# Copies of the normed rows made by TensorE from a twice-held transposed buffer, with six gathered rows in flight instead of seven

## The chip, the cores and the metric

The program runs on one core of one Trainium2 chip. The metric is the device time of one launch in microseconds (us), the lower the better. All numbers are float32.

## The reference

The kernel computes one step of a one-layer encoder on 1,024 prompt tokens and 32 sample tokens of width 1,024. A layer is attention of two kinds (stick-breaking over all earlier keys, and a 128-wide window), then a feed-forward part called PEER, in which each token picks 8 x 16 = 128 experts out of 16,384. An expert is one row of `u` and one row of `v`. Only PEER matters here:

```python
xn = rms_norm(h, g_ffn)                      # the normed rows
q  = (xn @ w_q).reshape(t, 8, 2, 128)        # queries of eight heads
s1, s2 = q[:, :, 0] @ keys_1.T, q[:, :, 1] @ keys_2.T
# top 16 of s1 and of s2, top 16 of their 256 sums -> idx (t, 8, 16), gate
hid = gelu(einsum('thkd,td->thk', u[idx], xn))
y   = einsum('thk,thkd->td', gate * hid, v[idx])
out = rms_norm(h + y, g_final)
```

## The kernel before, in words

A first phase (`projection_phase`) computes all projections and stores them in DRAM. The second phase (`fused_phase`) is what the change touches. It handles nine tiles of tokens, t = 0 to 8: eight of 128 prompt tokens and a last one of 32 sample tokens (rows of a tile that are shorter are held in four copies).

**The gathers.** `peer_uv` holds for each expert its row of `u` and its row of `v` side by side, 8 KB. One gather (L707, an indirect DMA issued by GpSimd) fetches 128 such rows, 1 MB, one per partition: 32 tokens times 4 of their experts. 32 gathers make a group g, which serves 32 tokens; there are 33 groups, so 1,056 gathers, four groups to a prompt tile. A gather lands in one of `RING` = 7 buffers `uv`.

**The life of a gathered buffer.** GpSimd issues gather n once the product that read gather n - 7 is done (`vmm`, L705). When it has landed, VectorE multiplies its `u` half with `x_rep` and sums (the dot, L893). After two dots ScalarE applies Gelu to them (L829) and writes two 32-column weight tiles `diag`, one per gather (L835). TensorE multiplies these with the `v` halves into `y_acc` (L1327), four matmul calls of 512 columns per pair. Only then is the pair of buffers free.

**`x_rep`.** The dot needs the group's 32 normed rows on all 128 partitions, four copies of each (`COPIES` = 4). Before, the normed rows `xn` are stored to the DRAM scratch `xn2` (L595) and read back by four DMAs of 32 rows for each group (`load_x_rep`, L602), into two buffers used in turn. The gain `g_ffn` is multiplied in on VectorE with a [128, 1024] copy of it that SyncE loads for every tile (L582) into the place of `kT` and `later`.

**The order of the work.** All engines run through the same written-out list of slots n, one slot per gather (`for n in range(FIRST_SLOT, LAST_SLOT)`, L858, L1101, L1334), and each does in each slot what tables such as `STEP_AT`, `ROUTE_AT` and `GROUP_AT` name. Beside the gathers of tile t, the slots hold the attention and the routing of tile t + 1: attention steps every 4 slots (2(t + 1) of them for a prompt tile, 17 for the last), each with scores, suffix sums and values on TensorE, exponentials and a logarithm on ScalarE (`weights`, L745; `softplus`, L731 to L735) and `keep` on VectorE; then windows and a tail (merge, output projection, norm, turning `xn` into `xnT`); then eight heads of routing, one every 12 slots (queries L1275, `exp_gate` L823 on ScalarE, top-16 searches on VectorE). Each engine works strictly in its own order, so a late instruction holds back all that stands behind it. SyncE issues the ordinary DMAs in the same way.

**ScalarE's tables.** An activation needs its function's table. Before, no table is asked for by the program in the slots; a load stands ahead of an activation whenever the table then held lacks its function. It loads for Exp (L745), for Ln after Exp (L735), for Exp in `exp_gate` (L823) and for Gelu (L829). A wait written in the program ahead of an activation is carried by the instruction that follows it.

**PSUM.** `o_sw` (512 columns) collects the window attention of a tile and is read by `merge_window` (semaphore `msw`); between tiles it is unused.

Of the kernel before, what the change touches and what calls it, by code (L numbers as in the profile page):

```python
# [13 lines left out]
P = 128  # L14
# [26 lines left out]
RING = 7  # L41
# [313 lines left out]
LAST_SLOT = GATHERS + 20  # L355
# [4 lines left out]
GROUP_AT = {(g + 1) * TS: g for g in range(GATHERS // TS)}  # L360
FINISH_AT = {min((t + 1) * P, GATHERS): t for t in range(NT + 1)}


def fused_phase(nc, io, w_q, w_out, s_w):

    with ExitStack() as ctx:
        def sb(name, shape, dt=F32):
# [12 lines left out]
        g_out = sb("g_out", [P, DK])  # L380
        g_final = sb("g_final", [P, DM])
# [14 lines left out]
        g_ffn = part(4, 6)  # L396
# [3 lines left out]
        xnT = sb("xnT", [P, DK, P])  # L400
# [38 lines left out]
                   msw ssq mean2 guess2 mA mB tm mTe op x_in h h_out ssh meanh guessh g_in xn xn_out tx xTe  # L439
# [4 lines left out]
        S_X = [sem(f"x_rep{i}") for i in range(2)]  # L444
# [43 lines left out]
        def _(sync):  # L488
# [5 lines left out]
            for k0, g in ((0, "norm_sb_out"), (4, "norm_swa_out")):  # L494
                sync.dma_start(g_out[:, k0:k0 + 4], io[g].rearrange("o (k p) -> p (o k)", p=P),
                               allow_slow_non_contiguous=True).then_inc(S["const"], 16)
# [83 lines left out]
            def load_g(t):  # L580
                hold(sync, S["pvw"], 4 * t + 4)
                sync.dma_start(g_ffn, io["norm_ffn"].partition_broadcast(P)).then_inc(S["g_in"], 16)  # L582

# [8 lines left out]

            def store_xn(t):
                hold(sync, S["xn"], t + 1)
                sync.dma_start(io["xn2"][tokens_of(t), :], xn[0:rows_of(t), :]).then_inc(S["xn_out"], 16)  # L595

            def load_x_rep(g):
                hold(sync, S["xn_out"], (g // 4 + 1) * 16)
                if g >= 2:
                    hold(sync, S["dot"], (g - 1) * TS)  # L600
                for c in range(COPIES):
                    sync.dma_start(x_rep[c * TS:(c + 1) * TS, g % 2, :], io["xn2"][g * TS:(g + 1) * TS, :]  # L602
                                   ).then_inc(S_X[g % 2], 16)

# [26 lines left out]
            for n in range(FIRST_SLOT, LAST_SLOT):  # L631
# [20 lines left out]
                if (at := WINDOW_AT.get(n - 7)) and at[1] == 3:  # L652
                    load_g(at[0])
# [4 lines left out]
                if (t := TAIL_AT.get(n - 19)) is not None:  # L658
                    store_xn(t)
                    if t == 0:  # L660
                        load_x_rep(0)
                        load_x_rep(1)
                        load_h(0)
                if (g := GROUP_AT.get(n - 2)) is not None and g + 2 < GATHERS // TS:
                    load_x_rep(g + 2)
                if (t := FINISH_AT.get(n - 14)) is not None:
                    store_y(t)
                    if t < NT:
                        load_h(t + 1)
# [7 lines left out]
        def _(pool):  # L677
            nc.gpsimd.memset(q_pad[:], 0.0).then_inc(S["zeroed"], 1)
            hold(pool, S["const"], 13 * 16)
# [32 lines left out]
        def _(act):  # L712
# [4 lines left out]

            def z_of(t, e):
# [3 lines left out]
            def softplus(t, e):  # L722
# [7 lines left out]
                view = soft[0:scores.shape[0], 0:scores.shape[1]]  # L730
                nc.scalar.activation(view, scores, ACT.Abs)  # L731
# [5 lines left out]
            def weights(t, e):  # L737
# [4 lines left out]
                if e == 0 and t:  # L742
                    act.wait_ge(S["xn_out"], t * 16)
                scores = z_of(t, e)
                nc.scalar.activation(probs[0:scores.shape[0], 0:scores.shape[1]], scores, ACT.Exp).then_inc(S["a"], 1)  # L745
# [28 lines left out]
            def merged_guess(t):  # L774
                rows = rows_of(t)
                act.wait_ge(S["mean2"], t + 1)
                rsqrt_guess(nc, act, stat[0:rows, 1, :], stat[0:rows, 2, :], stat[0:rows, 3, :]).then_inc(S["guess2"], 1)
# [13 lines left out]
            def h_guess(t):  # L791
                rows = rows_of(t)
                act.wait_ge(S["meanh"], t + 1)
# [624 lines left out]
```

## Time and profile before

| | |
|---|---|
| median of 3 runs | 3738.09 us (3716.6 to 3742.26) |
| profiled execution: its own time | 3744.33 us |
| profiled execution: span, first to last instruction | 3742.7 us |
| busy PE / DVE / ACT / POOL | 2630.0 / 2236.5 / 1467.8 / 1390.8 us |
| bytes moved, mean rate | 1236.71 MB, 330 GB/s |
| queue of the gathers / the ordinary DMAs | 1122.51 MB, 76.8% / 111.69 MB, 9.4% of 16 DMA engines' span |
| granted TensorE clock, mean | 0.825 of full |

The engines are PE (TensorE), PEld (its weight loads), DVE (VectorE), ACT (ScalarE), POOL (GpSimd) and SP (SyncE). "Busy" is time in which an instruction of the engine runs. "DMA share" is the mean busy share of the core's 16 DMA engines in a stretch; over short stretches it can come out slightly above 1. The first phase and the routing of the first tile end at about 459 us, when the first gather is issued; from there to the end the gathers run. In the page's division of the span in 40 slices, the DMA line shows 9 tenths or more in nearly every slice from about 650 us on.

### The profile page before, as it was taken

The page shows a single profiled execution, that of the slowest core. Times are in us where ns is not written, and L with a number is a line of the kernel's source. Part 1 is how long each engine was busy: PE and PEld are TensorE (multiplying, and loading weights), DVE is VectorE, ACT ScalarE, POOL GpSimd, SP SyncE. Part 2 cuts the span into 40 slices and gives each one's busy share as a digit, 9 for nine tenths or more (in the row PEclk, how much of TensorE's full clock was granted, in tenths as well). Part 3 has the DMA queues.
Part 4 walks back from the last instruction along what each step waited for, and adds up shares of the span by engine and source line. Part 5 has one row for each costly group of instructions (what it writes and reads, how often), then busy time and mean ns, then how long its engine had stood idle before and what let it go on. Part 6 is the DMA issues. An engine that isn't in the chain of part 4 may idle for free.

```text
span 3742.7 us, 40304 instructions
## 1 busy us (share of the span) xinstructions
PE 2630.0 (70%) x11692; PEld 1123.9 (30%) x11692; DVE 2236.5 (60%) x5671; ACT 1467.8 (39%) x3224; POOL 1390.8 (37%) x1363
## 2 busy tenths in 40 slices
PE   7997666667666875777677666776677766667665
PEld 4553442223222321232223222332233224322111
DVE  2010365676667666676576656775766665665675
ACT  1000134225423642364246524653466435552222
POOL 0000014444445344434433344344433433344443
PEclk9998778778878887887879788888888778778787
DMA  6222259999999999999999999999989999999997
GB/s 224 83 80 81 75 212 355 378 401 345 367 391 392 336 383 390 376 344 372 382 368 345 365 391 355 361 335 387 374 343 346 372 377 352 354 367 385 373 386 312
DMA packets 256792, 1236.71 MB, mean 330 GB/s; under 512 B 30304, under 2 KB 99712, under 8 KB 120384
## 3 DMA queue, kind: packets, MB, share of 16 engines
q0 software_dynamic: 156416, 1122.51, 76.8%
q1 hardware_dynamic: 100160, 111.69, 9.4%
q8 instruction: 91, 1.49, 0.2%
q14 instruction: 125, 1.02, 0.1%
HBM read 1205.98 MB, written 32.70 MB: 331 GB/s over the span
## 4 chain that ended last, share of the span: by engine, by line
PE 25%; DMA 22%; DVE 19%; issue 9%; ACT 7%; DVEq 4%; POOL 2%; ACTq 2%; SPq 0%; POOLq 0%
DMA f_uv<-peer_uv,f_idx 18%; PE f_y_acc L1327 12%; DVE f_uv L893 6%; PE f_q_ps L1275 4%; PE f_z L1252 4%; DMA f_work<-cache_sb_kT 3%; POOL f_uv L707 2%; ACT L829 1%; PE f_z L1165 1%; ACT f_diag L835 1%; DMA f_work<-scratch_nat 1%; ACT L735 1%; ACTq L732 1%; ACT L823 1%; ACTq L833 1%
## 5 line engine op out<-in xcount | busy, mean ns | idle before, releaser
L707 POOL DMA_INDIRECT f_uv<-peer_uv,f_idx x1056 | 1210.7, 1147 | 1866.6 <-PE f_y_acc L1327 1624.5
L1327 PE MATMUL f_y_acc<-f_uv,f_diag 128*32 128x512 f32 x4224 | 1318.0, 753 | 598.5 <-ACT f_diag L835 517.8
L893 DVE CUSTOM_DVE_ANT_0 f_uv<-f_uv,f_x_rep 128x1024 f32<-128x1024 f32 x1056 | 1292.8, 1227 | 696.5 <-DMA f_uv<-peer_uv,f_idx 690.7
L1327 PEld LDWEIGHTS f_y_acc<-f_uv,f_diag 128*32 128x32 f32 x4224 | 238.8, 125 | 1272.0 <-ACT f_diag L835 678.6
L829 ACT ACTIVATE f_act_hid<-f_hid 128x2 f32<-128x2 f32 x528 | 107.0, 203 | 1309.2 <-DVE f_hid L893 1293.8
L1275 PE MATMUL f_q_ps<-w_q,f_xnT 128*128 128x256 f32 x1152 | 286.4, 405 | 28.3 <-DVE f_cut L1013 24.4
L835 ACT ACTIVATE f_diag<-f_gate_fold,f_act_hid 128x32 f32<-128x32 f32 x1056 | 281.7, 313 | 38.6 <-issue 2.7
L283 PE MATMUL proj<-xnT,w_cols 128*128 128x512 f32 (+1 forms) x864 | 283.3, 491 | 2.1 <-DVE nat L251 1.6
L1275 PEld LDWEIGHTS f_q_ps<-w_q,f_xnT 128*128 128x128 f32 x1152 | 232.2, 205 | 117.1 <-issue 57.5
L829 ACT ACT_TABLE_LOAD x179 | 229.7, 1283 | 3.2
L691 POOL TENSOR_TENSOR f_gate_fold<-f_fold,f_gates 128x128 f32<-128x128 f32 x264 | 154.6, 585 | 129.1 <-DVE f_gates L1078 123.9
L1306 PE MATMUL f_sel_ps<-f_packed,f_ident 128*32 128x8 f32 x2112 | 37.8, 195 | 228.4 <-DVE f_packed L1068 192.5
L283 PEld LDWEIGHTS proj<-xnT,w_cols 128*128 128x128 f32 x864 | 143.4, 192 | 142.5 <-issue 141.8
L241 DVE TENSOR_SCALAR stage<-proj 128x512 f32<-128x512 f32 x18 | 12.4, 691 | 270.2 <-PE proj L283 270.2
L1252 PE MATMUL f_z<-w_out_sb,f_work 128*128 128x512 f32 (+1 forms) x288 | 145.4, 659 | 27.5 <-DVE f_work L980 27.5
L206 ACT ACTIVATE stage<-proj 128x512 f32<-128x512 f32 x18 | 10.8, 599 | 292.8 <-PE proj L283 292.8
L304 POOL DMA_DIRECT2D scratch_projT<-stage x18 | 10.0, 555 | 311.0 <-DVE stage L241 311.0
L745 ACT ACTIVATE f_work<-f_z 128x512 f32<-128x512 f32 (+2 forms) x89 | 49.5, 557 | 181.6 <-PE f_z L1172 142.5
L813 ACT ACTIVATE f_q<-f_q_ps 128x256 f32<-128x256 f32 x72 | 27.2, 378 | 230.7 <-PE f_q_ps L1275 230.7
L1306 PEld LDWEIGHTS f_sel_ps<-f_packed,f_ident 128*32 128x32 f32 x2112 | 31.3, 138 | 281.2 <-DVE f_packed L1068 277.0
L1315 PE MATMUL f_sel_ps<-f_y_part,f_fold 128*32 128x512 f32 x132 | 82.7, 713 | 45.9 <-DVE f_y L1085 22.9
L915 DVE SCALAR_TENSOR_TENSOR f_work<-f_z,f_work 128x512 f32<-128x512 f32 (+2 forms) x89 | 57.0, 640 | 92.5 <-ACT f_work L735 88.5
(154 smaller groups left out, 3082.9 us busy)
## 6 DMA issues: line engine op xcount, KB each, us to landing
f_x_rep<-scratch_xn SPq DMA_DIRECT2D x132, 128.0 KB
f_uv<-peer_uv,f_idx POOLq DMA_INDIRECT x1056
f_work<-scratch_projT SPq DMA_DIRECT2D x86, 128.0 KB
scratch_projT<-stage POOLq DMA_DIRECT2D x18, 528.0 KB, 3.9
w_cols<-w_in SPq DMA_DIRECT2D x18, 512.0 KB, 3.8
f_work<-scratch_nat SPq DMA_DIRECT2D x72, 128.0 KB
w_q<-w_peer_q SPq DMA_DIRECT2D x1, 8192.0 KB, 25.0
scratch_nat<-nat POOLq DMA_DIRECT2D x10, 512.0 KB, 3.4
```

The costliest lines, as they stand in the source:

```text
L283: last = nc.tensor.matmul(acc[s][:, a:b], w[:, s, k, :], xnT[:, k, a:b], start=(k == 0), stop=(k == DK - 1))
L691: nc.gpsimd.tensor_tensor(gate_fold[:, tick % 4, :, :], fold[:].unsqueeze(1).broadcast_to(full), gates[:, t % 2, head, j * PART:(j + 1) * ...
L707: pool.indirect_dma_start(uv[:, n % RING, :], None, io["peer_uv"], bass.IndirectOffsetOnAxis(ap=idx[:, t % 2, head, k:k + 1], axis=0),).th ...
L829: nc.scalar.activation(act_hid[:, tick % 2, first:first + 2], hid[:, tick % 4, first:first + 2], ACT.Gelu)
L835: made = nc.scalar.activation(diag[:, tick % 2, i, :], gate_fold[:, tick % 4, i, :], ACT.Copy, scale=act_hid[:, tick % 2, i:i + 1])
L893: nc.vector.tensor_tensor_reduce(row_u, row_u, x_rep[:, g % 2, :], 1.0, 0.0, ALU.mult, ALU.add, hid[:, tick % 4, n % PART:n % PART + 1]).t ...
L915: made = nc.vector.scalar_tensor_tensor(sp[0:keys, 0:width], z[0:keys, (e % 2) * 512:(e % 2) * 512 + width], 0.0, soft[0:keys, 0:width], A ...
L1252: last = nc.tensor.matmul(z[0:rows, b * 512:(b + 1) * 512], mergedT[:, k, 0:rows], w_out[:, k, b * 512:(b + 1) * 512], start=(k == 0), sto ...
L1275: last = nc.tensor.matmul(q_ps[:, 0:2 * QH], xnT[:, k, :], w_q[:, k, head * 2 * QH:(head + 1) * 2 * QH], start=(k == 0), stop=(k == DK - 1))
L1306: last = nc.tensor.matmul(sel_ps[c * TS:(c + 1) * TS, j * 8:(j + 1) * 8], ident[:, j * TS:(j + 1) * TS], packed[:, c * PART:(c + 1) * PART ...
L1315: nc.tensor.matmul(sel_ps[rows, :], fold[:], y_part[:, b * 512:(b + 1) * 512], start=True, stop=True, skip_group_check=True).then_inc(S["y ...
L1327: last = nc.tensor.matmul(y_acc[i * TS:(i + 1) * TS, b * 512:(b + 1) * 512], diag[:, tick % 2, i, :], uv[:, n % RING, DM + b * 512:DM + (b ...
```

## The change

`x_rep` is no longer loaded by DMA. TensorE makes the four copies from the transposed rows `xnT`: for each group and each half b of the columns, 16 matmul calls (4 blocks k, 4 copies c) with a 128x32 piece of `xnT` as the stationary operand and the 128x128 identity as the moving one, into `o_sw`; ScalarE then copies `o_sw` (128x512) to `x_rep` one slot later. This is done at slots 32(g - 1) and 32(g - 1) + 2, one group ahead of its use. `xnT` is held twice (`xnT[:, t % 2]`), because the copies of tile t's later groups are still to be made when tile t + 1 is turned. The gain `g_ffn` is now a [128, 8] column operand applied by ScalarE when it copies the turned rows, eight activations in place of one. The stores of `xn` to DRAM, the loads of `x_rep`, and the nine loads of `g_ffn` go. `RING` goes from 7 to 6. ScalarE's program asks for the table with both Exp and Ln (`log_table`) before the attention steps and the norms. The second half of a group's fold and addition moves two slots later, and so does what finishes a tile. Unchanged surroundings are cut:

```diff
-RING = 7
+RING = 6
 COPIES = P // TS
...
 GATHERS = (NT + 1) * P - 3 * TS
-LAST_SLOT = GATHERS + 20
+LAST_SLOT = GATHERS + 24
 STEP_AT = {step_slot(t, e): (t, e) for t in range(NT + 1) for e in range(steps_of(t))}
...
 GROUP_AT = {(g + 1) * TS: g for g in range(GATHERS // TS)}
+X_AT = {TS * (g - 1) + 2 * b if g else 2 * b - 18: (g, b) for g in range(GATHERS // TS) for b in range(2)}
 FINISH_AT = {min((t + 1) * P, GATHERS): t for t in range(NT + 1)}
...
         xn = part(2, 4)
-        g_ffn = part(4, 6)
         win = sb("win", [P, 6, 2])
...
         stat = sb("stat", [P, 6, 2])
-        xnT = sb("xnT", [P, DK, P])
+        xnT = sb("xnT", [P, 2, DK, P])
...
             sync.dma_start(sinks[:], io["swa_sinks"].partition_broadcast(P)).then_inc(S["const"], 16)
-            for k0, g in ((0, "norm_sb_out"), (4, "norm_swa_out")):
-                sync.dma_start(g_out[:, k0:k0 + 4], io[g].rearrange("o (k p) -> p (o k)", p=P),
+            for dst, g in ((g_out[:, 0:4], "norm_sb_out"), (g_out[:, 4:8], "norm_swa_out"), (g_ffn[:], "norm_ffn")):
+                sync.dma_start(dst, io[g].rearrange("o (k p) -> p (o k)", p=P),
                                allow_slow_non_contiguous=True).then_inc(S["const"], 16)
...
-            def load_g(t):
-                hold(sync, S["pvw"], 4 * t + 4)
-                sync.dma_start(g_ffn, io["norm_ffn"].partition_broadcast(P)).then_inc(S["g_in"], 16)
-
             def load_x(t):
...
                 sync.dma_start(io["h"][tokens_of(t), :], merged[0:rows_of(t), :]).then_inc(S["h_out"], 16)
-
-            def store_xn(t):
-                hold(sync, S["xn"], t + 1)
-                sync.dma_start(io["xn2"][tokens_of(t), :], xn[0:rows_of(t), :]).then_inc(S["xn_out"], 16)
-
-            def load_x_rep(g):
-                hold(sync, S["xn_out"], (g // 4 + 1) * 16)
-                if g >= 2:
-                    hold(sync, S["dot"], (g - 1) * TS)
-                for c in range(COPIES):
-                    sync.dma_start(x_rep[c * TS:(c + 1) * TS, g % 2, :], io["xn2"][g * TS:(g + 1) * TS, :]
-                                   ).then_inc(S_X[g % 2], 16)
...
                     load_window(at[0])
-                if (at := WINDOW_AT.get(n - 7)) and at[1] == 3:
-                    load_g(at[0])
                 if (t := TAIL_AT.get(n - 7)) is not None:
...
                     store_h(t)
-                if (t := TAIL_AT.get(n - 19)) is not None:
-                    store_xn(t)
-                    if t == 0:
-                        load_x_rep(0)
-                        load_x_rep(1)
-                        load_h(0)
-                if (g := GROUP_AT.get(n - 2)) is not None and g + 2 < GATHERS // TS:
-                    load_x_rep(g + 2)
-                if (t := FINISH_AT.get(n - 14)) is not None:
+                if TAIL_AT.get(n - 19) == 0:
+                    load_h(0)
+                if (t := FINISH_AT.get(n - 16)) is not None:
                     store_y(t)
...
+            table = ["log"]
+
+            def log_table():
+                if table[0] != "log":
+                    act.preload_act_table_set("natural_log_exp_and_others")
+                    table[0] = "log"
+
             def z_of(t, e):
...
                 view = soft[0:scores.shape[0], 0:scores.shape[1]]
+                log_table()
                 nc.scalar.activation(view, scores, ACT.Abs)
...
                 if e == 0 and t:
-                    act.wait_ge(S["xn_out"], t * 16)
+                    act.wait_ge(S["tx"], t)
                 scores = z_of(t, e)
+                log_table()
                 nc.scalar.activation(probs[0:scores.shape[0], 0:scores.shape[1]], scores, ACT.Exp).then_inc(S["a"], 1)
...
                 act.wait_ge(S["mean2"], t + 1)
+                log_table()
                 rsqrt_guess(nc, act, stat[0:rows, 1, :], stat[0:rows, 2, :], stat[0:rows, 3, :]).then_inc(S["guess2"], 1)
...
                 act.wait_ge(S["tx"], t + 1)
-                if t:
-                    act.wait_ge(S["q"], t * PH)
-                turned = z[:].rearrange("p (k t) -> p k t", k=DK)[:, :, 0:rows_of(t)]
-                if t < NT:
-                    nc.scalar.activation(xnT[:], turned, ACT.Copy).then_inc(S["xTe"], 1)
-                else:
-                    nc.scalar.activation(xnT[:].rearrange("p k (c t) -> p k c t", c=COPIES),
-                                         turned.unsqueeze(2).broadcast_to([P, DK, COPIES, TS]),
-                                         ACT.Copy).then_inc(S["xTe"], 1)
+                if t >= 2:
+                    act.wait_ge(S["q"], (t - 1) * PH)
+                    act.wait_ge(S["x_mm"], 8 * (t - 1))
+                for k in range(DK):
+                    turned, out = z[:, k * P:k * P + rows_of(t)], xnT[:, t % 2, k, :]
+                    if t == NT:
+                        turned = turned.unsqueeze(1).broadcast_to([P, COPIES, TS])
+                        out = out.rearrange("p (c t) -> p c t", c=COPIES)
+                    last = nc.scalar.activation(out, turned, ACT.Copy, scale=g_ffn[:, k:k + 1])
+                last.then_inc(S["xTe"], 1)
+
+            def copy_x(g, b):
+                act.wait_ge(S["x_mm"], 2 * g + b + 1)
+                if g >= 2:
+                    act.wait_ge(S["dot"], (g - 1) * TS)
+                nc.scalar.activation(x_rep[:, g % 2, b * 512:(b + 1) * 512], o_sw[:], ACT.Copy).then_inc(S["x_rep"], 1)
...
                 act.wait_ge(S["dot"], (batch + 1) * 2)
+                table[0] = "gelu"
                 nc.scalar.activation(act_hid[:, tick % 2, first:first + 2], hid[:, tick % 4, first:first + 2], ACT.Gelu)
...
                     group_out(g)
+                if (at := X_AT.get(n - 1)):
+                    copy_x(*at)
                 if (at := STEP_AT.get(n - 5)):
...
                 if n % TS == 0:
-                    dve.wait_ge(S_X[g % 2], (g // 2 + 1) * 16 * COPIES)
+                    dve.wait_ge(S["x_rep"], 2 * g + 2)
                 dve.wait_ge(S_UV[n % RING], (n // RING + 1) * 16)
...
                 if e == 0 and t:
-                    dve.wait_ge(S["xn_out"], t * 16)
+                    dve.wait_ge(S["tx"], t)
                 dve.wait_ge(S["ln"], s + 1)
...
                 dve.drain()
-                dve.wait_ge(S["g_in"], t * 16 + 16)
-                nc.vector.scalar_tensor_tensor(xn[0:rows, :], merged[0:rows, :], stat[0:rows, 5, 0:1], g_ffn[0:rows, :],
-                                               ALU.mult, ALU.mult).then_inc(S["xn"], 1)
+                nc.vector.tensor_scalar(xn[0:rows, :], merged[0:rows, :], stat[0:rows, 5, 0:1], None,
+                                        ALU.mult).then_inc(S["xn"], 1)
...
                         pe.wait_ge(S["msw"], t)
+                        pe.wait_ge(S["x_rep"], sum(slot < window_slot(t, 0) + 6 for slot in X_AT))
                 for i in range(2):
...
+            def copies_of_x(g, b, n):
+                t = g // 4
+                pe.wait_ge(S["xTe"], t + 1)
+                pe.wait_ge(S["msw"], sum(slot < n for slot in TAIL_AT))
+                if g or b:
+                    pe.wait_ge(S["x_rep"], 2 * g + b)
+                for k in range(4 * b, 4 * b + 4):
+                    for c in range(COPIES):
+                        last = nc.tensor.matmul(o_sw[c * TS:(c + 1) * TS, k % 4 * P:(k % 4 + 1) * P],
+                                                xnT[:, t % 2, k, g % 4 * TS:(g % 4 + 1) * TS], ident[:], start=True, stop=True,
+                                                skip_group_check=True)
+                last.then_inc(S["x_mm"], 1)
+
             def queries(r):
...
                 for k in range(DK):
-                    last = nc.tensor.matmul(q_ps[:, 0:2 * QH], xnT[:, k, :], w_q[:, k, head * 2 * QH:(head + 1) * 2 * QH],
+                    last = nc.tensor.matmul(q_ps[:, 0:2 * QH], xnT[:, t % 2, k, :], w_q[:, k, head * 2 * QH:(head + 1) * 2 * QH],
                                             start=(k == 0), stop=(k == DK - 1))
...
-                added = sum(slot + 4 + 2 * b < n for slot in GROUP_AT for b in range(2))
+                added = sum(slot + 4 + 4 * b < n for slot in GROUP_AT for b in range(2))
                 if routed:
...
                         project(t, quarter)
+                if (at := X_AT.get(n)):
+                    copies_of_x(*at, n)
                 for offset, stage in ((3, key_scores), (2, turn_queries), (0, queries)):
...
                 for b in range(2):
-                    if (g := GROUP_AT.get(n - 4 - 2 * b)) is not None:
+                    if (g := GROUP_AT.get(n - 4 - 4 * b)) is not None:
                         fold_group(g, b, n)
```

## Rows read from the trace of the kernel before

**Rows 1.** Stretches, gathers alone: us, busy (issues), PEclk, DMA share, GB/s
```profile
600.00:3400.00 2800.00, 1043.59 (x912) 0.82 0.96 367
3400.00:3700.00 300.00, 125.44 (x109) 0.77 0.99 385
```

**Rows 2.** The same, start to four instants: gathers issued
```profile
0.00:800.00 800.00, 119.19 (x99) 0.85 0.53 201
0.00:1600.00 1600.00, 428.18 (x367) 0.84 0.75 287
0.00:2400.00 2400.00, 723.37 (x625) 0.84 0.82 313
0.00:3200.00 3200.00, 1007.16 (x879) 0.83 0.85 325
```

**Rows 3.** Same instants, L893 on DVE, two instructions per dot
```profile
0.00:800.00 800.00, 118.80 (x194) 0.85 0.53 201
0.00:1600.00 1600.00, 445.96 (x724) 0.84 0.75 287
0.00:2400.00 2400.00, 767.06 (x1246) 0.84 0.82 313
0.00:3200.00 3200.00, 1076.37 (x1749) 0.83 0.85 325
```

**Rows 4.** 10 us around each: five engines, PEclk, DMA share, GB/s
```profile
795.00:805.00 10.00, 9.37 (x65) 4.29 (x66) 5.60 (x14) 1.92 (x8) 3.54 (x5) 0.83 1.02 360
1595.00:1605.00 10.00, 4.66 (x52) 2.02 (x50) 9.00 (x21) 7.62 (x13) 2.81 (x3) 0.83 1.02 415
2395.00:2405.00 10.00, 10.00 (x41) 6.12 (x39) 5.07 (x10) 6.99 (x11) 2.95 (x2) 0.91 0.64 234
3195.00:3205.00 10.00, 6.35 (x65) 2.52 (x60) 7.90 (x18) 7.65 (x14) 3.23 (x3) 0.67 1.02 398
```

**Rows 5.** Waits: waiting, waited for; us in total, times, longest
```profile
POOL f_uv L707 <- PE f_y_acc L1327: 1624.5, 413, 32.6
ACT f_act_hid L829 <- DVE f_hid L893: 1293.8, 346, 9.1
...
PE f_y_acc L1327 <- ACT f_diag L835: 517.8, 232, 6.5
...
ACT f_work L745 <- PE f_z L1172: 142.5, 53, 5.4
```

**Rows 6.** Timeline: start us, us, instruction, idle before
```profile
2318.87 1.85 POOL L707 DMA_INDIRECT f_uv<-peer_uv,f_idx  x1 [6.03 <-PE f_y_acc L1327]
...
2325.46 1.22 DVE L893 CUSTOM_DVE_ANT_0 f_uv<-f_uv,f_x_rep 128x1024 f32<-128x1024 f32 x1
```

**Rows 7.** DMA issues: engine, kind, times, KB each
```profile
f_x_rep<-scratch_xn SPq DMA_DIRECT2D x132, 128.0 KB
...
f_work<-norm_ffn SPq DMA_DIRECT2D x9, 512.0 KB
```

**Rows 8.** Timeline: bursts of matmul records on PE
```profile
2327.51 1.91 PE L1327 MATMUL f_y_acc<-f_uv,f_diag 128*32 128x512 f32 x8
...
2332.04 0.61 PE L1288 MATMUL f_q_ps<-f_keysT,f_qT 128*128 128x128 f32 x4
```

**Rows 9.** Groups of instructions: count, busy us, mean ns, idle before
```profile
L735 ACT ACT_TABLE_LOAD x83 | 106.5, 1283 | 4.9 <-issue 0.7
...
L823 ACT ACT_TABLE_LOAD x61 | 78.3, 1283 | 1.1
```

**Rows 10.** Timeline of ACT through one attention step
```profile
2317.26 1.28 ACT L745 ACT_TABLE_LOAD   x1
...
2321.06 0.60 ACT L745 ACTIVATE f_work<-f_z 128x512 f32<-128x512 f32 x1 [2.52 <-PE f_z L1172]
...
2322.90 1.28 ACT L735 ACT_TABLE_LOAD   x1
2324.19 0.63 ACT L735 ACTIVATE f_work<-f_work 128x512 f32<-128x512 f32 x1
```

More of the change, by code:

```diff
@@ L380, in fused_phase @@
         g_out = sb("g_out", [P, DK])
+        g_ffn = sb("g_ffn", [P, DK])
         g_final = sb("g_final", [P, DM])
@@ L438, in fused_phase @@
         names = """const zeroed keys_turn keys_copied z ln sp tri a pv kw dv zs nm p tp pTe pvw
-                   msw ssq mean2 guess2 mA mB tm mTe op x_in h h_out ssh meanh guessh g_in xn xn_out tx xTe
+                   msw ssq mean2 guess2 mA mB tm mTe op x_in h h_out ssh meanh guessh xn tx xTe x_mm x_rep
                    q qe qt qTe scores cut best gate_exp packed sel routed
@@ L443, in fused_phase @@
         S_UV = [sem(f"uv{i}") for i in range(RING)]
-        S_X = [sem(f"x_rep{i}") for i in range(2)]
         S_Q = [sem(f"q_pad{i}") for i in range(2)]
@@ L678, in _ @@
             nc.gpsimd.memset(q_pad[:], 0.0).then_inc(S["zeroed"], 1)
-            hold(pool, S["const"], 13 * 16)
+            hold(pool, S["const"], 14 * 16)
             def routed_by(tick):
@@ L793, in h_guess @@
                 act.wait_ge(S["meanh"], t + 1)
+                log_table()
                 rsqrt_guess(nc, act, stat[0:rows, 1, 0:1], stat[0:rows, 2, 0:1],
@@ L855, in guess @@
                 act.wait_ge(S["mean"], t + 1)
+                log_table()
                 rsqrt_guess(nc, act, y_stat[0:rows, 1:2], y_stat[0:rows, 2:3], y_stat[0:rows, 3:4]).then_inc(S["guess"], 1)
@@ L875, in _ @@
                         stage(at[0] * PH + at[1])
-                for offset, stage in ((9, square), (11, guess)):
+                for offset, stage in ((11, square), (13, guess)):
                     if (t := FINISH_AT.get(n - offset)) is not None:
@@ L883, in _ @@
         def _(dve):
-            dve.wait_ge(S["const"], 13 * 16)
+            dve.wait_ge(S["const"], 14 * 16)
             def dot(n):
@@ L1118, in _ @@
                 for b in range(2):
-                    if (g := GROUP_AT.get(n - 5 - 2 * b)) is not None:
+                    if (g := GROUP_AT.get(n - 5 - 4 * b)) is not None:
                         add(g, b)
-                for offset, stage in ((10, mean), (12, scale_y)):
+                for offset, stage in ((12, mean), (14, scale_y)):
                     if (t := FINISH_AT.get(n - offset)) is not None:
@@ L1126, in _ @@
         def _(pe):
-            pe.wait_ge(S["const"], 13 * 16)
+            pe.wait_ge(S["const"], 14 * 16)
             for f in range(2):
@@ L1374 @@
     "h": (TOK, DM),
-    "xn2": (TOK, DM),
 }
```

## The prediction

> **What bounds the kernel now.** I read three views in this order: the stretches of the gather phase, the counts of gathers and dots at instants, and the waits.
>
> The stretches say how near the DMA engines are to their limit. Between 600 and 3400 us 912 gathers are issued in 2800 us, 3.07 us each, at a DMA share of 0.96. After 3400 us, where no attention step is left, a gather takes 300/109 = 2.75 us at a share of 0.99 [rows 1]. So with attention beside it the kernel is close to the limit of the transfers but not at it: 4% of the DMA engines' time is lost.
>
> The counts say how that limit is held. A gather issued and not yet dotted is in the DMA engines or waits for VectorE. At 800, 1600, 2400 and 3200 us there are 99 - 97 = 2, 367 - 362 = 5, 625 - 623 = 2 and 879 - 874.5 = 4.5 of them [rows 2, 3]; the mean is 3.4. The DMA share around these instants is 1.02, 1.02, 0.64 and 1.02 [rows 4]. The reader is to see that the share is full with four or five gathers out, and that with two it may be full or fall to 0.64. The other 3.6 of the seven buffers are dotted and wait for Gelu, for TensorE or for GpSimd.
>
> The waits say what a gather waits for: 413 times for the product that frees its buffer, 1624.5 us in all [rows 5]. So the number of buffers decides when a gather is issued. One trip of a buffer takes 7 x 3.07 = 21.5 us: 3.4 x 3.07 = 10.4 us from issue to the end of the dot, 11.1 us from there to the next issue.
>
> **The change, part by part.**
>
> *Transfers taken out.* 132 loads of 128 KB, nine of 512 KB [rows 7], and the stores of 1,056 rows of 4 KB: 16,896 + 4,608 + 4,224 = 25,728 KB, 26.3 MB. At the 367 GB/s of the phase [rows 1] that is 72 us of full DMA time, 0.068 us per gather. Full DMA time per gather is now 0.96 x 3.07 = 2.95 us, and after it 2.88 us. If the share stayed at 0.96 the time would fall by 72 us. Ends: nothing (a transfer that fits into the idle 4%) and -72.
>
> *The seventh buffer.* This is the large term. If no part of the trip shrank, six buffers would give 21.5/6 = 3.58 us per gather: +0.51 x 1,056 = +539 us, the upper end. A part does shrink, the queue in front of the DMA engines and of the dot. Its size: with the DMA engines nearly empty the 600th gather, whose issue ends at 2320.7 us, is dotted from 2325.46 us, 4.7 us later [rows 6] (it is the 600th on both engines by counting). With the dot's 1.2 us that is 5.9 us against the mean of 10.4, so 4.5 us of the trip are queue. To stay at 3.07 us with six, a trip must fall to 18.4 us, so 3.1 of these 4.5 us must go, while the DMA engines are still 2.88/3.07 = 94% loaded. The issues come in pairs after gaps (6.03 us before the one in [rows 6]), and at the instant with two out the share was 0.64 already; with one buffer fewer the same gap in the returns leaves one out. So I do not expect 94%. The share lies between the 0.83 that [rows 4] give as the mean of the two instants with two out, and 0.96. Nearer to the upper end, because the trip gets shorter where the queue does and because the lowest two of four instants stand for the worst half: I take 0.91. Then a gather takes 2.88/0.91 = 3.165 us, +0.095 x 1,056 = **+100 us**, with the transfers' relief already in it. A trip is then 19.0 us, so 2.5 of the 4.5 us of queue go. Ends: 0.83 gives 3.47 us and +422; 0.96 gives 3.00 us and -72.
>
> *The copies on TensorE.* There are 66 bursts of 16 matmul calls, 32 records of 128 columns each. Four records of 128 columns take 0.61 us [rows 8], so 32 one after the other take 4.9 us. The pair's product shows overlap of two column groups: eight records of 512 columns in 1.91 us are 0.24 us each, where four times 0.15 would be 0.61, a factor 2.5 [rows 8]. I take 4.9/2.5 = 2.0 us a burst, 130 us in all; ends 1.2 us (four groups at once) and 4.9, twice that at the lower clock level. It lies on TensorE's order just behind the values and ahead of the next pair's product. 232 of the 528 pairs find TensorE waiting for ScalarE, 517.8 us in all [rows 5], so somewhat over half of the bursts push a pair back, by up to 2 us: 37 x 2.0 = 74 us of TensorE time, of which a trip over six buffers passes on a part. I take +25 us; ends 0 and +130.
> The trace shows two column groups overlapping by 2.5 and has no case of four full-size ones. The Trainium skill, page "TensorEngine Tiling (Array Packing)", section "Theoretical Speedup", gives up to four times for a free dimension of at most 32; by it a burst would take 1.2 us, and this term would be +15.
>
> *ScalarE.* Added: 66 copies of 128x512 at 0.60 us [rows 10], 40 us, and seven more small activations for each of nine tiles; between steps ScalarE waits for dots (1293.8 us over 346 of 528 pairs [rows 5]) and these hide there. If that cover were gone, 40 us at most. The copy stands one slot behind its burst, so ScalarE may wait for TensorE with the next Gelu behind it; the pair's diag is then late, and its buffers. Removed: the load for Ln behind Exp, 83 times, and most of the 61 loads of `exp_gate`, which stands behind a step's Ln in the same slot; 1.283 us each [rows 9], some 140 loads or 180 us busy. But the load ahead of `weights` moves. Now it starts at 2317.26 us, ahead of a wait, and the Exp starts at 2321.06 after 2.52 us of waiting for TensorE [rows 10]; the wait occurs 53 times [rows 5]. In the new program the wait stands ahead of the request for the table, so the load begins only when the wait is over. It costs 1.28 us there and saves 1.28 us behind: nothing for 53 of 83 steps. What is left is 30 steps and some 50 loads of `exp_gate`, 80 x 1.28 = 103 us, and a third of the pairs, at most, wait for ScalarE. I take -25 us; ends 0 and -103.
> After the load for Ln at 2322.90 the activation starts at 2324.19, 0.01 us after the load's end [rows 10]. The Trainium skill, page "ScalarE: Activation LUTs", section "What ACT_TABLE_LOAD costs", puts a drain of about 1.38 us on top of each load; by that rule this term would be some -50. The trace does not agree.
>
> *Waits and queues.* SyncE loses 132 + 9 + 9 DMAs and the holds ahead of them; it does not become later. The first step of each tile waits for the turned rows in place of the landing of the store of `xn`, which is earlier; worth a few us at most over eight tiles, taken as nothing, covered by the gathers' own trip. TensorE waits at the second burst of a group for ScalarE's first copy; behind it stands the next pair's product, which needs a later diag of ScalarE anyway. The end shifts by slots that hold no gather, so by nothing. The first tile pays two bursts and two copies on its way, some 5 us, against the store and the loads that fall away there.
>
> **Sum**, against the profiled execution (its own time 3744 us, its span 3742.7): 3744 + 100 + 25 - 25 = 3844 us. The median of the runs is 6 us below the profiled one, so I predict 3838 us.
>
> **The rivals.**
>
> *A, the forecast:* the lost buffer leaves the DMA engines waiting. For it: the share of 0.64 at the instant with two out, and the 413 waits on TensorE. Against it: 1.02 at the other such instant. 3775 to 3960 us.
>
> *B, the DMA relief decides (faster).* The queue is elastic enough: at 94% load the trip falls below 18.4 us, because each stall on ScalarE is shorter without the Ln load, and a dot waits less when fewer gathers have piled up. Its place is the trip, its price -72 us for the transfers and up to -25 for ScalarE: 3738 - 72 - 10 = about 3656 us, 3630 to 3700. It decides from the point where the share stays at or above 2.88/3.07 = 0.94. For it: the step-free stretch holds 0.99 with seven buffers [rows 1].
>
> *C, they cancel:* the share falls to 0.93 to 0.95, 3701 to 3775 us, no difference of over 1%.
>
> *D, the copies stall the order.* The bursts run at the lower clock level without overlap, 9.8 us, and ScalarE waits behind each with a Gelu. 66 x 5 us of it exposed, +330 us on top of the transfers' relief: 3738 - 72 + 330 = 3996 us. Against it: TensorE's idle time [rows 5].
>
> **How the numbers follow.** A 0.60, B 0.18, C 0.18, D 0.04. About 1% (37 us) is what a measurement of this kernel can tell from no change: faster 0.18, same 0.18, slower 0.64. The range for 8 in 10: down to 3690, which leaves out most of B, and up to 3960, which leaves out D and the far end of A's share. A's own range is 3775 to 3960.
>
> **What would show it.** In the new profile, DMA share from 600 to 3400 us near 0.91 and a gather at 3.15 to 3.2 us show the main step right; 0.94 or more shows B. Gathers out at instants should average about 2.5 to 2.9, not 3.4. Matmul bursts of 2 us into `o_sw`, and `x_rep` copies of 0.6 us with little wait, show the copies cheap. The Ln loads should be gone, and loads ahead of `weights` should start after its wait. In the step-free end the time per gather tells the buffer alone: 2.75 us if six suffice there, 2.9 or more if not. A trip whose part after the dot is well under 11 us would make the prediction wrong.

## The result, and the profile after

The changed kernel takes 3821.78 us (median of 4 runs, 3809.82 to 3844.44) against 3734.53 us for the kernel before in 4 runs: ratio 1.0248, 95% interval 1.0187 to 1.0309. It is slower by 2.5%; the forecast was 3838 us, with a range from 3690 to 3960. The profiled execution has a span of 3821.7 us, 79 us more than before.

The page after, its first part and the DMA part:
```profile
span 3821.7 us, 44416 instructions
PE 2735.3 (72%) x13804; PEld 1187.6 (31%) x13804; DVE 2235.7 (59%) x5671; ACT 1326.2 (35%) x3207; POOL 1396.7 (37%) x1363
DMA packets 249016, 1210.63 MB, mean 317 GB/s; under 512 B 28944, under 2 KB 98352, under 8 KB 112592
q0 software_dynamic: 156416, 1122.51, 76.3%
q1 hardware_dynamic: 92368, 85.34, 6.9%
```
The 26 MB are gone from the ordinary queue (111.69 MB before). TensorE has 105 us more to do, ScalarE 142 us less. And yet the mean rate falls from 330 to 317 GB/s: the DMA engines have less to move and stand idle for longer.

The gathers by stretch, the same columns as [rows 1]:
```profile
600.00:3400.00 2800.00, 1020.45 (x897) 0.83 0.93 353
3400.00:3700.00 300.00, 116.36 (x101) 0.75 0.93 352
```
A gather takes 2800/897 = 3.12 us in place of 3.07, at a DMA share of 0.93 in place of 0.96; in the stretch without attention steps 2.97 us at 0.93 in place of 2.75 us at 0.99. Full DMA time per gather is 0.93 x 3.12 = 2.90 us (2.95 before).

The first hundred gathers lose the most for their number. They take 342 us before (the first of the two lines) and 367 after, at a DMA share of 0.85 and 0.81:
```profile
459.00:801.00 342.00, 120.02 (x100) 0.79 0.85 329
```
```profile
460.00:827.00 367.00, 110.25 (x100) 0.77 0.81 306
```
Of the 79 us between the two profiled executions, 25 lie there, 39 in the next 860 gathers and 13 in the last 96; the rest is spread over start and end.

The waits, as in [rows 5]; the third line stands for the kernel before at 690.7 us in 469 waits:
```profile
POOL f_uv L683 <- PE f_y_acc L1338: 1727.1, 436, 45.0
ACT f_act_hid L824 <- DVE f_hid L891: 1575.0, 412, 12.0
DVE f_uv L891 <- DMA f_uv<-peer_uv,f_idx: 948.8, 609, 7.0
PE f_y_acc L1338 <- ACT f_diag L830: 636.0, 250, 7.9
ACT f_x_rep L801 <- PE f_o_sw L1272: 55.7, 15, 7.1
```
The reader is to see that every engine of the buffer's trip waits more, VectorE for landings above all: the gathers come too late. The last line is what ScalarE waits for the copies, 15 times; whether it costs time is for e4 to say.

What the change put in, from the groups of instructions (busy us, mean ns, idle before):
```profile
L1272 PE MATMUL f_o_sw<-f_ident,f_xnT 128*32 128x128 f32 x2112 | 85.4, 285 | 11.6 <-ACT f_x_rep L801 11.6
L801 ACT ACTIVATE f_x_rep<-f_o_sw 128x512 f32<-128x512 f32 x66 | 38.6, 585 | 55.7 <-PE f_o_sw L1272 55.7
L794 ACT ACTIVATE f_xnT<-f_z,f_g_ffn 128x128 f32<-128x128 f32 x72 | 19.4, 376 | 3.8 <-PE f_z L1260 3.8
```
A burst takes 85.4/66 = 1.3 us, not the 2.0 I took, and a copy 0.585 us, as forecast.

ScalarE's table loads, by line, in the changed kernel:
```profile
L824 ACT ACT_TABLE_LOAD x171 | 219.4, 1283 | 3.1
L698 ACT ACT_TABLE_LOAD x116 | 148.8, 1283 | 139.6 <-PE f_z L1169 110.9 <-PE f_z L1165 14.4 <-DVE f_y_stat L1087 8.6
L736 ACT ACT_TABLE_LOAD x32 | 41.1, 1283 | 0.6
L817 ACT ACT_TABLE_LOAD x31 | 39.8, 1283 | 0.5
```
And one attention step whose load stands behind the wait, with no load ahead of the Ln in L719:
```profile
2430.82 1.28 ACT L698 ACT_TABLE_LOAD   x1 [3.04 <-PE f_z L1169]
2432.11 0.60 ACT L730 ACTIVATE f_work<-f_z 128x512 f32<-128x512 f32 x1
2432.60 0.59 ACT L715 ACTIVATE f_work<-f_z 128x512 f32<-128x512 f32 x1
2433.26 0.63 ACT L717 ACTIVATE f_work<-f_work 128x512 f32<-128x512 f32 x1
2433.96 0.63 ACT L719 ACTIVATE f_work<-f_work 128x512 f32<-128x512 f32 x1
2434.61 1.28 ACT L824 ACT_TABLE_LOAD   x1
```
The loads for Ln (83) are gone and those of `exp_gate` fell from 61 to 31 [rows 9]; the remaining ones ahead of a step that waits now begin when the wait is over, unlike in [rows 10]. Gone too are 50 loads of the norms, which the kernel before has in the first guess of the inverse root (a Ln, then an Exp); the requests at L698 stand for them now:
```profile
L71 ACT ACT_TABLE_LOAD x25 | 32.1, 1283 | 0.4
L73 ACT ACT_TABLE_LOAD x25 | 32.1, 1283 | 1.3
```

### The profile page after: what moved, and what is told of

It is laid out like the page before. It is cut to its first block, busy times and chain, and to the rows that moved or that the text cites. A ratio compares the mean times of both kernels' runs of the same rounds, so it can differ in the third digit from the quotient of the medians.

```text
span 3821.7 us, 44416 instructions
## 1 busy us (share of the span) xinstructions
PE 2735.3 (72%) x13804; PEld 1187.6 (31%) x13804; DVE 2235.7 (59%) x5671; ACT 1326.2 (35%) x3207; POOL 1396.7 (37%) x1363
## 4 chain that ended last, share of the span: by engine, by line
PE 29%; DMA 28%; DVE 17%; issue 6%; DVEq 5%; ACT 2%; POOL 2%; ACTq 1%; SPq 0%; POOLq 0%
DMA f_uv<-peer_uv,f_idx 23%; PE f_y_acc L1338 13%; DVE f_uv L891 6%; PE f_q_ps L1286 6%; DMA f_work<-cache_sb_kT 4%; PE f_z L1250 4%; POOL f_uv L683 2%; DVEq L1056 1%; DVEq L1043 1%; DVE f_pick L1053 1%; DVE f_pick L1050 1%; PE f_z L1162 1%; PE f_z L1143 1%; DVE f_chosen L1057 1%; ACT f_diag L830 1%
## 5 line engine op out<-in xcount | busy, mean ns | idle before, releaser
L1338 PE MATMUL f_y_acc<-f_uv,f_diag 128*32 128x512 f32 x4224 | 1338.1, 766 | 678.7 <-ACT f_diag L830 636.0
L1286 PE MATMUL f_q_ps<-w_q,f_xnT 128*128 128x256 f32 x1152 | 294.2, 413 | 27.6 <-DVE f_cut L1010 24.8
L667 POOL TENSOR_TENSOR f_gate_fold<-f_fold,f_gates 128x128 f32<-128x128 f32 x264 | 171.0, 648 | 121.6 <-DVE f_gates L1075 116.4
L1186 PEld LDWEIGHTS f_o_sb<-f_work 128*128 128x128 f32 (+2 forms) x848 | 89.9, 171 | 60.5 <-ACT f_work L730 40.0
L1143 PE MATMUL f_z<-f_q_pad,f_work 128*128 128x256 f32 x288 | 101.9, 487 | 1.0 <-DMA f_work<-scratch_projT 1.0
L1186 PE MATMUL f_o_sb<-f_work 128*128 128x64 f32 (+2 forms) x848 | 100.8, 267 | 1.0 <-ACT f_work L730 0.7
```

The lines of the kernel that those rows point to most:

```text
L667: nc.gpsimd.tensor_tensor(gate_fold[:, tick % 4, :, :], fold[:].unsqueeze(1).broadcast_to(full), gates[:, t % 2, head, j * PART:(j + 1) * ...
L1143: last = nc.tensor.matmul(z[:, at:at + 256], kT[:, (e % 2) * 256 + m * P:(e % 2) * 256 + (m + 1) * P], q_pad[:, f, m, :, :].rearrange("p a ...
L1186: last = nc.tensor.matmul(o_sb[0:n, hd * HD:(hd + 1) * HD], probs[0:keys, i * n:(i + 1) * n], v_blk[0:keys, col:col + HD], start=(e == 0 a ...
L1286: last = nc.tensor.matmul(q_ps[:, 0:2 * QH], xnT[:, t % 2, k, :], w_q[:, k, head * 2 * QH:(head + 1) * 2 * QH], start=(k == 0), stop=(k == ...
L1338: last = nc.tensor.matmul(y_acc[i * TS:(i + 1) * TS, b * 512:(b + 1) * 512], diag[:, tick % 2, i, :], uv[:, n % RING, DM + b * 512:DM + (b ...
```

## The experiments

Ratios are to the kernel before, timed on the same chip beside each. That kernel's median moves from 3734.53 to 3744.11 us between the chips, so a difference between rows that have another time beside them is good to some 10 us; where it matters, the ratios are compared.

| run | buffers | median us | before beside it | ratio, 95% interval |
|---|---|---|---|---|
| changed kernel | 6 | 3821.78 | 3734.53 | 1.0248, 1.0187 to 1.0309 |
| e1, before with six | 6 | 3950.98 | 3743.48 | 1.0546, 1.0513 to 1.0578 |
| e2, change with seven, stand-in gain | 7 | 3637.61 | 3743.48 | 0.9712, 0.9680 to 0.9745 |
| e3, change, table request first | 6 | 3828.05 | 3743.48 | 1.0229, 1.0198 to 1.0259 |
| e4, change, copies left out | 6 | 3831.01 | 3743.48 | 1.0215, 1.0167 to 1.0262 |
| e5, before, no `x_rep` loads | 7 | 3711.92 | 3740.72 | 0.9923, 0.9902 to 0.9943 |
| e6, before, table requests | 7 | 3703.74 | 3740.72 | 0.9899, 0.9878 to 0.9921 |
| e7, change with seven, true output | 7 | 3638.11 | 3740.72 | 0.9720, 0.9687 to 0.9753 |
| e8, change with five | 5 | 4199.09 | 3740.72 | 1.1227, 1.1198 to 1.1256 |
| e9, before, all those transfers out | 7 | 3699.21 | 3744.11 | 0.9878, 0.9850 to 0.9906 |
| e10, e7 without table requests | 7 | 3702.38 | 3744.11 | 0.9894, 0.9872 to 0.9916 |
| e11, e7, table request first | 7 | 3630.94 | 3744.11 | 0.9698, 0.9677 to 0.9720 |
| e12, change without table requests | 6 | 3907.80 | 3736.82 | 1.0465, 1.0441 to 1.0490 |

**e1, the buffer alone.**
```diff
-RING = 7
+RING = 6
```


> The kernel before with six gathered rows and nothing else changed. Theory (the lost buffer decides, relief of the transfers works against it): full DMA time per gather stays 2.95 us, the DMA share falls to about 0.92 to 0.93 as in the changed kernel, so 3.19 us per gather, about +130 us, 3830 to 3900 us, slower than the changed kernel. Rival (the copies on TensorE and ScalarE cost the time, the buffer is spare): within 20 us of the kernel before, 3715 to 3755 us.

Measured: +207 us, above what I expected (3830 to 3900 us). The stretches:
```profile
600.00:3400.00 2800.00, 996.56 (x860) 0.82 0.92 345
3400.00:3700.00 300.00, 105.13 (x93) 0.76 0.93 350
```
2800/860 = 3.26 us per gather at a share of 0.92; the share was as expected, but full DMA time per gather is 3.00 us and not 2.95. The second line isn't step-free here: this run is later, with attention steps to 3462 us and window steps to 3517. Its stretch without either is
```profile
3550.00:3850.00 300.00, 119.99 (x98) 0.74 0.93 349
```
which is 3.06 us per gather against 2.75. The rival, a spare buffer, falls.

**e2, the change with its buffer given back.** A seventh buffer is 8 KB per partition; with what is free already, the 4 KB of the held final gain make room for it.
```diff
-RING = 6
+RING = 7
...
-        g_final = sb("g_final", [P, DM])
+        g_final = w_out[:, 0, :]
```


> The changed kernel with seven gathered rows. To make room, the [128,1024] copy of the final gain is left out and the last norm multiplies with a slice of w_out of the same size, so the outputs y are scaled by other numbers; count and size of all operations stay. Theory: DMA share back at 0.96 or above from 600 to 3400 us, full DMA time 2.90 us per gather, so about 3.0 us per gather and 3650 to 3690 us, faster than the kernel before by 1.5 to 2%. Rival (copies cost it): still 3780 us or more.

Measured: 3637.61 us, 106 us less than the kernel before, slightly below the range expected and far from the rival. The same six rows that make the change slower hide a change that makes it faster.
```profile
600.00:3400.00 2800.00, 1106.54 (x949) 0.85 0.95 373
```
2.95 us per gather at a share of 0.95, full DMA time 2.80 us.

**e3, the request for the table ahead of the waits**, in all five functions that have one.
```diff
             def weights(t, e):
                 s, f, b = step(t, e)
+                log_table()
                 act.wait_ge(S["tri"], s + 1)
...
-                log_table()
                 nc.scalar.activation(probs[0:scores.shape[0], 0:scores.shape[1]], scores, ACT.Exp).then_inc(S["a"], 1)
```


> The changed kernel with each request for the log and exp table put ahead of the waits of its function instead of behind them. Theory: 53 or so loads of 1.28 us no longer stand behind a wait for TensorE; pairs come to Gelu up to 1.28 us earlier behind those steps; with six buffers that is 10 to 40 us less than the changed kernel: 3780 to 3812 us. Rival (ScalarE is off the trip, DMA share alone sets the time): no difference beyond 5 us.

Measured: 3828.05 us, 6 us from the change and inside its interval (1.0229 and 1.0248). The loads did move; the wait now stands with the activation:
```profile
L698 ACT ACT_TABLE_LOAD x116 | 148.8, 1283 | 2.0
L730 ACT ACTIVATE f_work<-f_z 128x512 f32<-128x512 f32 (+2 forms) x89 | 49.5, 556 | 81.3 <-PE f_z L1169 58.7 <-PE f_z L1165 22.1
```
So it makes no measurable difference whether a load stands ahead of such a wait or behind it. The theory falls. The rival has the number, but its reason, that ScalarE is off the trip, does not hold (e12).

**e4, the copies left out** but for the first two groups.
```diff
-X_AT = {TS * (g - 1) + 2 * b if g else 2 * b - 18: (g, b) for g in range(GATHERS // TS) for b in range(2)}
+X_AT = {TS * (g - 1) + 2 * b if g else 2 * b - 18: (g, b) for g in range(2) for b in range(2)}
```


> The changed kernel with only the first two of 33 groups' copies made; the other 62 bursts on TensorE and their copies on ScalarE are left out (the dots use old rows, outputs y are wrong). Six buffers. Theory: the copies are nearly hidden, so 5 to 30 us less than the changed kernel, 3792 to 3817 us. Rival (copies cost the time): 60 us or more less, 3760 us or below.

Measured: 3831.01 us, not less than with them. On the same chip e3, which makes the copies, took 3828.05. By the ratios e4 is 12 us below the change, with 29 us of uncertainty either way. So the 62 bursts and their copies cost nothing that this run can tell from nothing; 60 us or more, the rival, is excluded. The 5 to 30 us of the theory are not shown and, by the ratios, not excluded. e9 and e10 settle it more closely.

**e5, the largest of the transfers out of the kernel before.**
```diff
-                if (g := GROUP_AT.get(n - 2)) is not None and g + 2 < GATHERS // TS:
+                if (g := GROUP_AT.get(n - 2)) is not None and g + 2 < 2:
```


> The kernel before, seven buffers, with only the first two groups' x_rep loads; the other 124 DMAs of 128 KB are left out and the dots use old rows (outputs y are wrong). The stores of xn and the loads of the gain stay. The two runs at seven buffers showed 106 us between the kernel before and the changed one where 26.3 MB at 367 GB/s are 72 us. Theory (bytes): 16.3 MB of the 26.3 go, so 44 us less, 3685 to 3710 us. Rival 1 (these small loads cost more than their bytes, since they come as a burst of four while gathers queue): 65 us or more less, 3680 us or below. Rival 2 (the table loads make the difference): under 30 us less.

Measured: -29 us (-37 to -21 by the interval), less than the 44 by bytes. The theory by bytes falls and so does rival 1; rival 2 has the number. The relief turns into idle DMA engines, the share falls from 0.96 to 0.93:
```profile
600.00:3400.00 2800.00, 1059.13 (x922) 0.82 0.93 365
```

**e6, the table requests alone in the kernel before**, in the same five functions as in the change; one of them is shown.
```diff
+                log_table()
                 nc.scalar.activation(view, scores, ACT.Abs)
```


> The kernel before, seven buffers, x_rep by DMA, with the change's requests for the log and exp table alone. Theory (what is above the bytes in the 106 us comes from ScalarE): 20 to 40 us less than the kernel before, 3700 to 3725 us. Rival (ScalarE's loads are off the trip, as moving them made no difference with six buffers): within 10 us of the kernel before.

Measured: -37 us, in the range of the theory. The profiled execution was the slowest of the four (3720.52 us); it has 3.04 us per gather, and the share stays at 0.96:
```profile
600.00:3400.00 2800.00, 1060.20 (x920) 0.83 0.96 370
```

**e7, a version with seven buffers and the true output.** The final gain is loaded into `y_part` for each tile, between the squares and the last scaling.
```diff
+            def load_final_gain(t):
+                hold(sync, S["squares"], t + 1)
+                sync.dma_start(y_part[0:rows_of(t), :], io["norm_final"].partition_broadcast(rows_of(t))
+                               ).then_inc(S["g_late"], 16)
...
-                for offset, stage in ((12, mean), (14, scale_y)):
+                for offset, stage in ((12, mean), (17, scale_y)):
```


> The changed kernel with seven buffers and the true output: the final gain is no longer held but loaded for each tile into y_part between the squares and the last scaling, nine DMAs of at most 512 KB (4.3 MB, 12 us at 367 GB/s), and the scaling moves three slots later. Theory: the run with seven buffers and a stand-in for the gain (3638 us) plus 5 to 20 us, 3640 to 3660 us, faster than both kernels. Rival (the wait for the gain stalls VectorE in its order, nine times some 8 us, and the end of the last tile): 3700 us or more.

Measured: 3638.11 us, faster than the kernel before by 2.8% (0.9687 to 0.9753) and than the changed one by 4.8%. The late gain costs nothing beside e2.

**e8, five buffers.**
```diff
-RING = 6
+RING = 5
```


> The changed kernel with five buffers. Theory (a trip of the buffer sets the time as the queue is used up): seven, six buffers gave 2.95 and 3.12 us per gather with trips of 20.6 and 18.7 us; five leave at most another 1.5 us to shrink, so 17.2 to 17.7 us a trip, 3.45 to 3.55 us per gather, 4150 to 4280 us. Rival (each buffer costs the same 184 us): 4000 to 4020 us.

Measured: 4199.09 us, in the range of the theory.
```profile
600.00:3400.00 2800.00, 888.14 (x806) 0.80 0.85 316
```
3.47 us per gather, a trip of 5 x 3.47 = 17.4 us. Seven, six and five buffers give 3638, 3822 and 4199 us: +184, then +377. The rival of a fixed price falls.

**e9, all the transfers out of the kernel before**, nothing in their place: the edit of e5, and
```diff
-                if (at := WINDOW_AT.get(n - 7)) and at[1] == 3:
+                if (at := WINDOW_AT.get(n - 7)) == (0, 3):
                     load_g(at[0])
...
-                if (t := TAIL_AT.get(n - 19)) is not None:
+                if (t := TAIL_AT.get(n - 19)) == 0:
                     store_xn(t)
```


> The kernel before, seven buffers, with all that the change takes out of the transfers left out and nothing put in: x_rep loads only for the first two groups, the gain loaded and xn stored for the first tile alone, and the waits for those stores become waits for the turned rows, as in the change (outputs y are wrong). Table loads as before. Theory (transfers and tables add up to the change at seven buffers, 106 us, of which tables are 37): about 70 us less than the kernel before, 3660 to 3685 us. Rival (the two together give more than their sum, since each alone leaves the other as the limit): 3690 to 3710 us.

Measured: -45 us, 3699 us: the rival. Transfers alone 45 us, tables alone 37 us, the two together 106 us in e2 and 103 in e7. The excess over the sum is 22 to 25 us by the ratios, with some 18 us of uncertainty.

**e10, e7 without the table requests.**
```diff
-                log_table()
```


> The true kernel with seven buffers (final gain loaded late), with the requests for the log and exp table taken out, so that Exp and Ln load a table each as before. Theory: the requests are worth here what they are worth alone in the kernel before, 37 us: 3660 to 3690 us. Rival (they matter less where the transfers are relieved): 3640 to 3655 us.

Measured: 3702.38 us, 64 us more than e7; outside both ranges, on the side of the sum that is more than its parts. It is level with e9 (3699.21), the same chip: 3 us more, 6 by the ratios, with 13 of uncertainty. e10 makes the copies, applies the gain on ScalarE and has the later slots of the fold and of the end; e9 has none of these. With seven buffers all of them together cost next to nothing.

**e11, e7 with the request ahead of the waits** (the edit of e3).

> The true kernel with seven buffers, with each request for the table ahead of the waits of its function. With six buffers this made no difference. Theory: none here either, 3630 to 3648 us. Rival (with seven buffers pairs reach ScalarE earlier and find it busy more often, so 1.28 us at some 50 steps show): 3600 to 3625 us.

Measured: 3630.94 us, 0.9698 against 0.9720 for e7, within each other's intervals: the theory.

**e12, the change without its table requests** (the edit of e10, six buffers).

> The changed kernel, six buffers, with the requests for the log and exp table taken out (each Exp and Ln loads its own table as before). Theory (with the transfers relieved ScalarE's loads lie on the trip, and with six buffers a longer trip costs at least as much as with seven, where it was 64 us): 60 to 90 us more than the changed kernel, 3880 to 3915 us. Rival (my sum's -25 us was right for six buffers): 3840 to 3855 us.

Measured: 3907.80 us, 86 us more than the change (81 by the ratios, with 25 of uncertainty), as the theory has it. My sum's -25 us is shown wrong.
```profile
600.00:3400.00 2800.00, 990.36 (x872) 0.83 0.90 344
```

## Why the prediction came out right, and where it did not

The direction and the main mechanism came out: the lost buffer lengthens the wait for a free buffer, and the relief of the transfers does not make up for it. The total came out too, forecast +100 us, measured +87 (79 between the profiles), but by luck: the runs give the 87 us other terms than mine, and the errors cancel.

**The seventh buffer decides.** It is worth 207 us in the kernel before (e1), 205 between e10 and e12, 184 between e7 and the change. Rival B, that the DMA relief decides, had its condition at a share of 0.94; the share came out at 0.93, and at 0.90 without the table requests. B is what happens with seven buffers. Rival C had the share right, 0.93 to 0.95, and the time wrong (3701 to 3775 us): a share from 600 to 3400 us says little of the 25 us that the first hundred gathers lose. My own sum did not price them apart either.

**The term of buffer and transfers was mis-sized.** I had +100 us for the two. The runs with table loads as before give 3908 - 3737 = +171 us (e12, 163 between the profiles). What was too small is the time per gather, from a share of 0.91: the share was 0.90 and the gather took 2800/872 = 3.21 us instead of 3.165, which over 1,056 gathers is +48 us. Most of the rest lies at the start: the first hundred gathers of e12 take 367 us against 342, 25 us more, where 3.21 us a gather covers 14.
```profile
463.00:830.00 367.00, 114.56 (x100) 0.80 0.81 305
```

**The table term was mis-sized the other way**, -25 us in the sum and -86 measured with six buffers (e12). The number of loads came out for the wrong reason: about 140 forecast, 146 fewer by count (498 before, 352 after). I had most of the 61 of `exp_gate` going, and 30 went; I had overlooked the 50 of the norms. The step that failed is the cancelling: I wrote that a load behind a wait costs 1.28 us there, which eats up the load for Ln that is saved behind it, for 53 of 83 steps. e3 and e11 move these loads ahead of the wait, and the time moves by 6 us up and 7 us down, inside the intervals. So the cost there is not seen, and with it falls the reason to count 80 loads only, and a quarter of their 103 us. By the runs 146 loads less are worth 86 us, 0.6 us a load on average. How this divides between the steps that wait and the others is open; no run takes loads out of the one kind alone.

Where the 86 us go in the trip can be read from the trace. The times below are means over every gather that was issued from 600 us on and whose buffer was issued again before 3400 us, from the end of the issue on GpSimd to the end of the dot on VectorE, and from there to the end of the next issue into the same buffer.

| run | buffers | trip, us | issue to end of dot | behind the dot | gathers out |
|---|---|---|---|---|---|
| before | 7 | 21.5 | 11.0 | 10.5 | 3.6 |
| changed kernel | 6 | 18.8 | 9.2 | 9.6 | 2.9 |
| e12, change without table requests | 6 | 19.3 | 9.3 | 10.0 | 2.9 |

The table requests take 0.5 us from the trip, 0.4 of it behind the dot, where ScalarE's Gelu stands. The trip shrank by 2.8 us from before to the change, where my sum had 2.5: 1.9 us out of the queue and 0.9 behind the dot. I had all of it from the queue.

**The copies on TensorE**: +25 us in the sum, nothing that could be told from nothing (e4), and next to nothing with seven buffers (e10 against e9). The burst was priced at 2.0 us and takes 1.3. The Trainium skill's figure, which gave 1.2 us (page "TensorEngine Tiling (Array Packing)", section "Theoretical Speedup"), was the better one. A factor of 2.5 from two column groups was a sign by itself that 0.15 us overstates what a record takes, and so that the 4.9 us are too high. Rival D falls with it.

So 171 - 86 + 0 = 85, against my 100 - 25 + 25. The errors are 71 us too little for buffer and transfers, 61 too little relief for the tables and 25 too much for the copies.

**The transfers.** 26.3 MB were priced at 72 us. Alone they are worth 45 us (e9), with the tables 106 - 37 = 69. I had named the possibility that a transfer fits into the 4% idle DMA time, and not followed it: e5 shows it in part, as the share drops from 0.96 to 0.93.

**What I said the profile would show.** Share near 0.91: 0.93. A gather at 3.15 to 3.2 us: 3.12. Step-free end at 2.9 or more: 2.97. Fewer gathers out, 2.5 to 2.9: 2.9 by the mean over all gathers. The four instants don't show it. At them issues and dots after are
```profile
0.00:800.00 800.00, 101.43 (x92) 0.86 0.51 187
0.00:1600.00 1600.00, 402.86 (x354) 0.84 0.72 271
0.00:2400.00 2400.00, 692.27 (x606) 0.84 0.78 297
0.00:3200.00 3200.00, 979.33 (x861) 0.84 0.82 311
```
```profile
0.00:800.00 800.00, 109.79 (x178) 0.86 0.51 187
0.00:1600.00 1600.00, 431.82 (x699) 0.84 0.72 271
0.00:2400.00 2400.00, 745.62 (x1206) 0.84 0.78 297
0.00:3200.00 3200.00, 1059.96 (x1714) 0.84 0.82 311
```
which leaves 3, 4.5, 3 and 4 out, a mean of 3.6 against 3.4 before. Taken at their word they would put the part behind the dot at 18.7 - 3.6 x 3.12 = 7.5 us, well under 11, and that was my sign of being wrong. The mean over all gathers is 9.6 us, from 10.5. Four instants are too few to tell a shift of half a gather.

## What to carry to other kernels

Where one engine waits for a ring of buffers and the transfers are near their limit, multiply buffers by time per item to get the trip, find how much of it is queue, and ask whether a lost buffer can come out of that alone. Take how much is queue from all items, not from a few instants. The price of a buffer grew with each one taken here: 184 us for the seventh, 377 for the sixth. Price a second saving together with the first: transfers and table loads gave 45 and 37 us alone and 106 together. That each alone leaves the other as the limit is my reading of it: with the transfers alone gone the DMA share fell to 0.93 (e5, e9), with both it stayed at 0.95 to 0.96 (e2, e7). And look for the room first: 4 KB per partition, held for a gain that is read nine times, were worth 184 us as a part of a buffer.

## What the runs showed of the hardware

- Matmuls into four different 32-column groups, 128 columns each, overlap: 32 records take 1.17 us.
```profile
2121.02 1.17 PE L1272 MATMUL f_o_sw<-f_ident,f_xnT 128*32 128x128 f32 x32 [1.64 <-ACT f_x_rep L801]
```
One after the other, at the 0.15 us a record of [rows 8], it would be 4.9 us by my estimate. That is more than four times 1.17, so the 0.15 us, from a burst of four records, is on the high side.
- A table load is 1.283 us and no more: the activation after the load at 2430.82 begins at 2432.11, with no drain between. The load at 2434.61 begins 0.02 us after the activation ahead of it has ended. The Trainium skill, page "ScalarE: Activation LUTs", section "What ACT_TABLE_LOAD costs", adds about 1.38 us; neither trace agrees.
- All DMA traffic of the core, the gathers and the ordinary transfers beside them, comes to 373 GB/s with seven buffers, 353 with six and 316 with five from 600 to 3400 us, the program the same but for the final gain in e2 (e2, the change, e8).
